# Two-layer mixer and expert network on one core: out-projection, norm and first queries tile by tile

## What is computed

```python
mix = jnp.concatenate([pool_x, attn_x, ml_x], axis=-1) @ w_out[l]
x = x + g_a * mix
x = x + g_f * peer_ffn(modulate(x, norm2_gain[l], sh_f, sc_f), peer_wq[l], peer_subkeys[l], peer_u[l], peer_v[l])

def peer_ffn(h, w_q, subkeys, u_tab, v_tab):            # for a block of P tokens
    q = (hb @ w_q).reshape(P, PEER_HEADS, 2, PEER_DKEY // 2)
    s = jnp.einsum('phcd,hcnd->phcn', q, subkeys)
    top_v, top_i = lax.top_k(s, PEER_TOPK)
    cand = top_v[:, :, 0, :, None] + top_v[:, :, 1, None, :]
    best, flat = lax.top_k(cand.reshape(P, PEER_HEADS, 256), PEER_TOPK)
    expert = i1 * PEER_KEYS + i2                        # from top_i and flat
    g = jax.nn.softmax(best, axis=-1)
    a = jax.nn.gelu(jnp.einsum('pd,phkd->phk', hb, u_tab[expert]))
    return jnp.einsum('phk,phkd->pd', (g * a), v_tab[expert])
```

## Time and profile before

| what | value |
|---|---|
| time, median of three | 2670.63 us |
| span of the profiled execution (first to last instruction) | 2664.6 us |
| TensorE (PE) busy | 2150.9 us, 81% |
| VectorE (DVE) busy | 1636.1 us, 61% |
| ScalarE (ACT) busy | 1140.6 us, 43% |
| GpSimd (POOL) busy | 810.0 us, 30% |
| read from HBM | 937.26 MB, 352 GB/s over the span |
| gathers (q0) | 805.36 MB, 73.0% of the DMA engines' time |
| weight loads (q1) | 130.31 MB, 12.4% |
| granted TensorE clock | 0.949 of full |

### The profile page before, as it was taken

How to read it: one execution, slowest core, us unless ns; L and a number is a source line. 1 busy time by engine, 2 the same in 40 slices (tenths; PEclk the granted TensorE clock), 3 DMA queues, 4 the chain that set the end, 5 groups by cost and what they waited for, 6 DMA issues and landing times.

```text
span 2664.6 us, 26635 instructions
## 1 busy us (share of the span) xinstructions
PE 2150.9 (81%) x8372; PEld 1003.3 (38%) x8372; DVE 1636.1 (61%) x4029; ACT 1140.6 (43%) x3280; POOL 810.0 (30%) x772
## 2 busy tenths in 40 slices
PE   6899889876788677796677777789989987777776
PEld 3667745432344243351122111166774321221111
DVE  1125376687887665766677666445536666677654
ACT  3144264555774434455333333335423333443332
POOL 0000033443445334333434333200004444343331
PEclk8999999978999889998899999999899999999999
DMA  7667199999999999999999999922019999999997
GB/s 302 255 247 316 34 397 412 396 362 392 407 399 405 421 414 412 418 419 421 422 421 422 421 422 421 412 89 76 36 34 392 425 426 426 425 426 426 426 426 308
DMA packets 133660, 940.05 MB, mean 353 GB/s; under 512 B 14864, under 2 KB 16144, under 8 KB 23312
## 3 DMA queue, kind: packets, MB, share of 16 engines
q0 software_dynamic: 110592, 805.36, 73.0%
q1 hardware_dynamic: 22496, 130.31, 12.4%
q10 hardware_dynamic: 432, 2.70, 0.3%
HBM read 937.26 MB, written 1.05 MB: 352 GB/s over the span
## 4 chain that ended last, share of the span: by engine, by line
DMA 45%; PE 33%; DVE 10%; ACT 7%; issue 3%; POOL 1%; SPq 0%; DVEq 0%; POOLq 0%; ACTq 0%
DMA fast<-uv_dram,idx 27%; DMA mix<-uv_dram,idx 14%; PE bank L1816 11%; PE bank L1775 5%; PE bank L1534 4%; DVE fast L1400 4%; PE bank L1739 2%; DMA qring<-wq_dram 2%; DMA fast<-w_dram 2%; PE bank L1499 2%; PE bank L1528 1%; PE bank L1784 1%; ACT diag L973 1%; ACT coef L970 1%; PE bank L1506 1%
## 5 line engine op out<-in xcount | busy, mean ns | idle before, releaser
L1816 PE MATMUL bank<-fast,diag 128*64 128x512 f32 x1956 | 797.0, 653 | 247.4 <-ACT diag L973 242.5
L667 POOL DMA_INDIRECT fast<-uv_dram,idx x489 | 525.8, 1075 | 1395.0 <-PE bank L1816 695.1
L1400 DVE SCALAR_TENSOR_TENSOR fast<-fast,hrow 128x1024 f32<-128x1024 f32 x489 | 598.3, 1224 | 347.9 <-DMA fast<-uv_dram,idx 342.2
L969 ACT ACTIVATE gact<-araw 128x1 f32<-128x1 f32 x768 | 154.5, 201 | 904.3 <-DVE fast L1400 548.2
L1816 PE MATMUL bank<-mix,diag 128*64 128x512 f32 x816 | 387.4, 628 | 99.3 <-ACT diag L973 96.5
L1816 PEld LDWEIGHTS bank<-fast,diag 128*64 128x64 f32 x1956 | 190.5, 144 | 706.6 <-ACT diag L973 454.3
L1400 DVE SCALAR_TENSOR_TENSOR mix<-mix,hrow 128x1024 f32<-128x1024 f32 x204 | 250.0, 1226 | 178.3 <-DMA mix<-uv_dram,idx 174.0
L667 POOL DMA_INDIRECT mix<-uv_dram,idx x204 | 203.4, 997 | 291.7 <-PE bank L1816 270.2
L973 ACT ACTIVATE diag<-con,coef 128x64 f32<-128x64 f32 x768 | 267.1, 348 | 25.1
L970 ACT ACTIVATE coef<-gact,wts 128x1 f32<-128x1 f32 x768 | 226.2, 295 | 24.9
L1816 PEld LDWEIGHTS bank<-mix,diag 128*64 128x64 f32 x816 | 93.2, 139 | 341.2 <-ACT diag L973 224.7
(11 more groups left out here) (265 smaller groups left out, 2588.6 us busy)
## 6 DMA issues: line engine op xcount, KB each, us to landing
fast<-w_dram SPq DMA_DIRECT2D x72, 1024.0 KB, 8.9
qring<-wq_dram SPq DMA_DIRECT2D x40, 576.0 KB
back<-w_dram SPq DMA_DIRECT2D x20, 1024.0 KB
fast<-uv_dram,idx POOLq DMA_INDIRECT x489
mix<-wq_dram SPq DMA_DIRECT2D x8, 576.0 KB, 5.6
mix<-uv_dram,idx POOLq DMA_INDIRECT x204, 27.5
fast<-uq_dram SPq DMA_DIRECT2D x4, 576.0 KB, 3.8
xT<-x_dram ACTq DMA_DIRECT2D x1, 2048.0 KB, 8.6
```

The source lines that it names most:

```text
L667: g.indirect_dma_start(slot(e, m), None, uv_tabs[e], bass.IndirectOffsetOnAxis(idx[:, Q % 2, n:n + 1], 0)).then_inc(landed[place], 16)
L969: link(a.activation(gact[:, n:n + 1], araw[:, Q % 2, n:n + 1], ACT.Gelu))
L1400: v.scalar_tensor_tensor(out=u, in0=u, scalar=1.0, in1=hrow[:, (2 * i + half) % 3, :], op0=ALU.mult, op1=ALU.mult, accum_out=araw[:, Q % 2 ...
L1816: mm = t_.matmul(acc[half, f * 512:(f + 1) * 512], diag[:, j % DIAGS, :], slot(e, j)[:, D + f * 512:D + (f + 1) * 512], start=(j % SLOTS < ...
```

## The change

In mixers alone (0 and 3) the 256 tokens fall into `parts`: tile A (`j = 0`) and tile B (`j = 1`). Out-projection, residual, squares, norm and modulation are made for A, then for B, with 128 columns each. Blocks of A come each 2 slots from 129 on; B's first four from 146, its last four from 168, among the turns of rows. The w_out tiles stay until B's blocks are done.

The requests for choices get numbers n of their own (`ASKS`): units 0 to 3 for A, units 4 to 7 for both tiles, units 0 to 3 for B, then units 8 on for both. The first four (`first_asks`) and the first two heads' choice (`first_choice`) are parts of the mixer now, from `ASK_AT` = 154 on. Units 4 to 7 move behind the first gathers, to slots 0 to 7, units 0 to 3 for B to slots 8 to 11, units 8 to 15 from slots 0 to 47 to slots 12 to 59. The next two heads' choice moves from slots 0 to 21 to slots 9 to 26, its weights' exponential from 23 to 28. In layer 0 the mixer behind starts three slots later (`BEHIND_AT`).

Units 0 to 3 are loaded to more_q, 4 and 5 to qring. GpSimd's wait for the residual is gone. Four of the six fast places hold w_out; a gather that takes one first waits for the last product of B with it. In layer 0 the seventh place is there from slot 72 on. In layer 1 three of the six places in mix can be used from slot 26 on, after B's requests.

```diff
+def parts(p):
+    return ((0,), (1,)) if alone(p) else ((0, 1),)
+def out_at(p, j, b):
+    if not alone(p):
+        return TIMES[p].out + OUT_STEP * b
+    if j == 0:
+        return TIMES[p].out + HALF_STEP * b
+    return TIMES[p].out + 17 + HALF_STEP * b if b < 4 else ASK_AT + 14 + HALF_STEP * (b - 4)
...
+def ask_list(e):
+    first = [(u, A_TILE) for u in range(FIRST)]
+    first += [(u, BOTH) for u in range(FIRST, 8)] + [(u, B_TILE) for u in range(FIRST)]
+    return first + [(u, BOTH) for u in range(8, HC * len(STREAMS[e]))]
...
-    window(0, 8, 2)
-    window(16, 12, 1)
+    window(0, range(4, 8), 0, 4)
+    window(8, range(FIRST), 1, 8)
+    window(12, range(8, 12), 0, 2)
+    window(28, range(12, 16), 0, 1)
...
-                    if 2 <= u < 6:
+                    if u < FIRST:
                         sp.wait_ge(attn_out.sem, attn_out.at(3 * e, 8))
...
-                g.wait_ge(x_mid.sem, x_mid.at(3 * e, KC))
...
-            def out_products(p):
+            def out_products(p, j):
+                cs = span(parts(p)[j])
...
-                            mm = t_.matmul(bank[b % 2][:, 0:SEQ], w[:, k, b % 2 * P:b % 2 * P + P], own_h(p)[:, k, :],
+                            mm = t_.matmul(bank[b % 2][:, cs], w[:, k, b % 2 * P:b % 2 * P + P], own_h(p)[:, k, cs],
...
+            def first_asks(p):
+                e = PHASES[p][0]
+                for at, n in ((0, 0), (2, 1), (4, None), (5, 2), (7, None), (8, 3), (10, None), (12, None)):
+                    yield ASK_AT + at
+                    if n is None:
+                        key_scores(e, {4: 0, 7: 1, 10: 2, 12: 3}[at])
+                    else:
+                        query(e, n, 0, KC)
+                for half in range(2):
+                    for f in range(2):
+                        yield ASK_AT + 13 + 4 * half + 2 * f
+                        rows_turn(e, 0, half, f)
...
+            def first_choice(p):
+                for H in range(2):
+                    for step in range(11):
+                        yield ASK_AT + 14 + 11 * H + step
+                        retrieve(PHASES[p][0], H, step)
...
+                                steps_now = range((n - 9) * 22 // 18, (n - 8) * 22 // 18) if 9 <= n < 27 else ()
```

More of the change, by code:

```diff
@@ L124, in row_at, with ask_of, window @@
     return TIMES[p].rows[j]
+FIRST = 4
+A_TILE, B_TILE, BOTH = (0,), (1,), (0, 1)
+def ask_list(e):
+    first = [(u, A_TILE) for u in range(FIRST)]
+    first += [(u, BOTH) for u in range(FIRST, 8)] + [(u, B_TILE) for u in range(FIRST)]
+    return first + [(u, BOTH) for u in range(8, HC * len(STREAMS[e]))]
+ASKS = [ask_list(e) for e in range(2)]
+def ask_of(e, u, t):
+    return next(n for n, (unit, ts) in enumerate(ASKS[e]) if unit == u and t in ts)
 def query_steps(e):
     steps = []
-    def window(slot, unit, per):
-        for j in range(4):
+    def window(slot, units, t, per):
+        for u in units:
@@ L144, in query_steps, with fast_uses @@
     return steps
 MIX_W = 7504
[L150 to L154, removed]
+def fast_uses(e, out_places):
+    slots_ = P * len(TILES[e])
+    free = [s for s in range(FAST) if s not in out_places]
+    return [("fast", s, 0, slots_, None) for s in free], [("fast", s, 0, slots_, f"out{b}") for b, s in enumerate(out_places)]
@@ new lines, in uses @@
+def uses(e, out_places):
+    free, held = fast_uses(e, out_places)
+    if e == 0:
+        at = BEHIND_AT + 180
+        return free + held + [("query", 0, 72, 196, "queried"), ("ctx", 0, 134, 266, "turned"), ("ctx", 0, 312, 512, "projected"),
+                              ("mix", 5448, at, 512, "attended"), ("mix", MIX_W, at, 262, "attended"),
+                              ("mix", MIX_W + BIG, at, 262, "attended"), ("mix", MIX_W, 336, 512, "rows"), ("mix", MIX_W + BIG, 336, 512, "rows")]
+    mixes = [("mix", BIG * s, 0, 256, None) for s in range(3)] + [("mix", BIG * s, 26, 256, "asked") for s in range(3, 6)]
+    return free + [("ctx", 0, 0, 256, None)] + mixes[0:3] + held + mixes[3:]
@@ L168, in ring_table @@
     return table
-RINGS = [ring_table(e) for e in range(2)]
+RINGS = [ring_table(0, (4, 0, 1, 2))]
 def freed(e, m):
@@ L246 @@
         PLACES[_u[:3]] = (_ring, _s, _uses[_s])
+RINGS.append(ring_table(1, tuple(PLACES[(3, "out", b)][1] for b in range(OUT_TILES))))
+assert [PLACES[(0, "out", b)][1] for b in range(OUT_TILES)] == [4, 0, 1, 2]
 def load_order():
@@ L941, in keys, with asked @@
-            def keys(e, u):
+                             row_turned(p), exponentials(p), prob_turned(p), *[norm2(p, j) for j in range(len(parts(p)))], *[first_asks(p)] * alone(p))
+            def asked(e, n):
+                a.wait_ge(pq_mm.sem, pq_mm.at(e, n + 1))
+                if n >= 2:
+                    a.wait_ge(psc_mm.sem, psc_mm.at(e, n - 1))
+                src = bank[3] if n < FIRST and n % 2 else b_query
+                cs = span(ASKS[e][n][1])
+                a.activation(pq[:, n % 2, cs], src[:, cs], ACT.Copy).then_inc(pq_ready.sem, 1)
@@ L1099, in norm1 @@
                 v.memset(v1[:, :, :, MD:MD + 1], 1.0).then_inc(pad_done.sem, 1)
+            def norm1(p):
                 yield 6
```

308 lines of the change are left out of this document (161 added, 147 removed).

## The result

The changed kernel takes 2696.2 us (median; 2690.2 to 2698.8) against 2671.6 before (2668.5 to 2673.1, with a fourth execution beside the three whose median was 2670.63): ratio 1.0086, 95% interval 1.0071 to 1.0101. It is 24.6 us slower; I had forecast 2667, and 2681 as the upper end. The profiled execution took 2698.6 us.

A forecast was written before the change was run, and what follows sets the result against it. Bound: first mixer, gathers at DMA's byte rate, last mixer, gathers. Each start 15 us earlier, mostly given back to bytes, TensorE backlog and reload waits, leaves 2 + 2 = 4 us off the median 2670.6: 2667 us, range 2652 to 2681.

The forecast's parts named there:

- The start: Out-projection to second head's gathers, both lone mixers: 63.9 us instead of 80.2; taken as 15 us earlier each, range 12 to 17.
- the fourth rival: Half-width products cost as much as whole ones because the weight load shows: 2727 us, chance 0.02.
- Layer 0's sum to slot 27: Layer 0: 15 us earlier, 1.9 of bytes back, less 8.8 backlog, 4 reload waits, 2.5 loads and seventh place: about 2 gained.
- The 1.9 us of bytes: Layer 0: part of 2.9 us for two moved query reloads, back since the second gather no longer shares with query loads.
- three slots less of the mixer behind, -4.0: TensorE backlog in layer 0 to slot 27: later mixer 1 removes three slots of work, some 1.3 us each.
- Layer 1: TensorE finishes slot 15 after 76 us, DMA idles some 10: 15 - 2.9 - 10 = 2 us gained.
- Reload waits: TensorE waiting for units 6 and 7, slots 4 and 6: 2 us each in layer 0, 3.5 in layer 1.
- the half clock: Second rival's term: slots 0 to 2 at about 1.2 GHz, 10 us of products costing 5 more.
- My sign for it: DMA share under 0.9 in the 40 us after the first gathers, both layers; 1.0 would mean the forecast was too slow.
- four rivals: Start kept, 2658 (0.34); backlog outweighs it, 2679 (0.19); second head only 8 us earlier, 2681 (0.05); half-width full cost, 2727 (0.02).
- the second: Rival: TensorE's backlog, with half clock and longer reloads, costs more than the start gains: 2679 us, chance 0.19.
- The seventh place at slot 72: Layer 0 gather place opening at slot 72 instead of 52: within about 2.5 us shared with loads still due at slot 27.

The follow-up runs named there:

- shift 0: Changed kernel with mixer 1 starting at slot 0 again instead of slot 3, rest of the change kept: 2672.2 us, ratio 1.0002 to the kernel before.
- the shift alone: Kernel before with only mixer 1 starting three slots later, its load windows and query steps going with it: 2687.3 us, ratio 1.0063.
- Shifts of 2 and 3 with odd scores: Changed kernel with mixer 1 two slots later instead of three: 2679.3 us; with three kept and attention one slot later, scores at odd slots: 2676.9 us.
- The run without these loads: Changed kernel with mixer 1 at slot 0, query-weight loads of units 6 and 7 left out in layer 1 alone: 2662.8 us, ratio 0.9964.
- the version that beats both: Changed kernel, mixer 1 at slot 0, units 4 and 5 asked and scored and reloads issued before the first slot, later steps rearranged: 2652.5 us, ratio 0.9928.

## Why the prediction was wrong, point by point

**The start: right in kind, 3.5 us too small.** A half block with its square took 2.01 us where I had taken 1.95 + 0.24 = 2.19 (0.112 us an instruction, under all the rows I had gone by); the start took 61.6 us instead of 63.9, against a cautious 65. The rule of the Trainium skill (TensorE: Matmul & The Clock Gate, The mechanism) behind the fourth rival, by which the weight load would show at half width, isn't borne out: by it a half block would have taken 3.4 us, as I had estimated, and block and square took 2.01.

**Layer 0's sum to slot 27: too small, hidden by the start.** I had counted 15 us gained and 13.4 of them given back by slot 27. The 1.9 us of bytes stand in that sum as a gain, and there they belong: the dots are 20.5 us early at slot 0 and 22.8 at slot 6. With shift 0 the pair of slots 26 and 27 ends at 426.4 us, where 425.9 was to be met within 3; that is 18.5 + 0.5 = 19 us given back, not 13.4. In the changed kernel it ends at 429.8, 0.9 outside, with its gathers 20.5 us early on the clock of the trace: 20.5 + 3.9 = 24.4 us given back. The term "three slots less of the mixer behind, -4.0" isn't borne out in this kernel. In the traces mixer 1's sums filled TensorE's wait for unit 6 (2.0 us with shift 0, 5.34 with shift 3), and moved out of it they came on top of the backlog; in the kernel before, where that wait isn't there, the dots are indeed 1.4 to 4 us earlier at slots 26 to 30 with the shift alone. Shifts of 2 and 3 with odd scores cost 7 and 5 us by the medians; how much of it arises here, a single trace of each doesn't show.

**Layer 1: about right, by luck, for two errors that cancel.** With shift 0 TensorE finishes slot 15 at 78 us after the second head's gathers (76 forecast), and DMA stands idle 7 us from 2020 to 2070 (10 forecast, though my own terms, 76 + 2.5 - 67, give 11.5). Reload waits were taken at 3.5 us each and measured 5.25 and 4.25 (4.59 and 4.81 in the changed kernel), and the half clock behind them, 3.4 us, I had weighed only for the first slots. The start's extra 3.5 made up for it. The run without these loads puts the whole at 10 us. My sign for it, a DMA share under 0.9 in the 40 us behind the first gathers, came 40 us late in the changed kernel:

```profile
2020.00:2060.00 40.00, 30.23 (x93) 16.52 (x95) 11.10 (x18) 8.02 (x29) 14.40 (x13) 0.84 1.00 415
2060.00:2100.00 40.00, 39.67 (x181) 22.07 (x178) 26.80 (x82) 14.35 (x52) 15.08 (x12) 0.99 0.84 300
```

The gathers already queued keep DMA full while TensorE waits; the gap shows when they are used up. I had written that a share of 1.0 in those 40 us would mean a faster kernel; it didn't.

**The step that failed.** I priced the shift by the work that it moves out of the first 27 slots, and followed it no further. Its cost lies 100 slots on, in another stage of mixer 1: some 2.4 us for each of eight heads, 19 us, where I had put it at nothing. Without it the changed kernel takes 2676.9 us (measured, with the scores at odd slots), inside the range and within 6 us of the kernel before. None of my four rivals is this one; the second has the right sign, but not the cause: backlog, half clock and waits took back what the start had gained, and no more; the 24.6 us are the attention's parity (19) and the rest of what the shift costs (5 to 7).

**The seventh place at slot 72:** priced near nothing, measured 2 us by the medians, 4 at most. Right.

## What to carry to other kernels

Where an order is written by hand and some steps come in pairs, a shift of whole slots isn't neutral: look where each step of the shifted part stands against the pair in every stage, and shift by even numbers. A long wait is no cost by itself: taking away 25.8 us of VectorE's gave nothing, while taking away two waits of TensorE of 5 us, which the ring of gathers waits for, gave 10. Idle time before the first value product is the place for anything that releases a load. And one trace of each kernel doesn't place a difference of a few us: two traces of the same code in layer 0 lay 10 us apart at slot 130.

## What the runs showed of the hardware

In layer 1 a load of 0.59 MB issued while gathers are queued took 8.0 to 9.0 us (shift 0), and kept TensorE waiting for 4 to 5 us even though one query product and one value product lay in between; leaving two such loads out of layer 1 gave 10 us, of which their bytes are 2.8. Behind such gaps TensorE ran at the lower level of its clock: products of 1.99 us took 3.51 to 3.78 after waits of 4.3 to 5.3 us (shift 0 and the changed kernel), but 1.99 after waits of 0.9 and 2.1 (the version that beats both). In the attention's stretch from 760 to 820 us the granted clock was 0.86 to 0.91 in the changed kernel, where TensorE had to wait, and 1.00 in it with odd slots (1.00, 1.00 and 0.91 in the kernel before). A stall like the reloads' costs its length and then the slower products behind it. With 128 columns and 128x128 weights in fp32 products followed one another at 0.112 us, half of the 0.216 at 256 columns.
